# A decoder layer with a retrieval FFN on one core: second-pass products behind the V sums, adaLN on 32-column tiles, a later cache fetch, longer rings, samples as a unit

## The reference

```python
sh1,sc1,g1,sh2,sc2,g2 = split6(silu(c) @ w_ada + b_ada)     # adaLN, c: 1 prompt row + 8 sample rows
h  = RMSNorm(x)*(1+sc1)+sh1
q,k,v,p,ga,gb = split(h @ w_in)                             # (520 tokens, 1024) @ (1024, 3328)
A  = window_attention(q, k, v)                              # window 128; samples: 128 cached keys each
B  = multiscale_pool(p)
x  = x + g1 * ((sigmoid(ga)*(A@w_a) + sigmoid(gb)*(B@w_b)) @ w_out)
h2 = RMSNorm(x)*(1+sc2)+sh2
# PEER: 8 heads; 16 of 128*128 experts per token and head
s_half, i_half = top_k(h2 @ w_q . sub_keys, 16)             # two halves of 128 keys
best, expert   = top_k(all 16x16 sums, 16)
act = gelu(h2 . u_tab[expert])                              # one row of 1024 per expert
x  = x + g2 * sum_over_heads_and_slots(softmax(best) * act * v_tab[expert])
```

## Time and profile before

| | before |
|---|---|
| median of 3 runs (lowest to highest) | 2025.64 us (2020.49 to 2031.15) |
| profiled execution, its own time | 2020.82 us |
| its span, first to last instruction | 2018.8 us |
| granted clock of TensorE, mean | 0.825 of full speed |
| busy: PE, DVE, POOL, ACT | 68%, 55%, 54%, 13% |
| DMA: moved, mean rate | 639.19 MB, 317 GB/s |

### The profile page before, as it was taken

How to read it: one execution, slowest core, us unless ns; L and a number is a source line. 1 busy time by engine, 2 the same in 40 slices (tenths; PEclk the granted TensorE clock), 3 DMA queues, 4 the chain that set the end, 5 groups by cost and what they waited for, 6 DMA issues and landing times.

```text
span 2018.8 us, 19410 instructions
## 1 busy us (share of the span) xinstructions
PE 1379.0 (68%) x7019; PEld 677.7 (34%) x7019; DVE 1108.1 (55%) x2614; ACT 257.1 (13%) x488; POOL 1093.1 (54%) x1066
## 2 busy tenths in 40 slices
PE   5799889998687766555887555555565555654577
PEld 2256746757344443232443111121111112111122
DVE  4111324137865665756466676667777765776521
ACT  2012531112111100111111000001000000100020
POOL 2100000005766657567477777757777775777772
PEclk9899899899798978778898667777666777678899
DMA  9422332469999989979699999989999998999994
GB/s 273 110 88 94 107 83 85 156 241 332 354 380 401 357 339 382 367 279 393 247 384 379 406 406 409 401 332 408 358 408 405 406 399 326 407 406 402 409 372 171
DMA packets 196264, 639.19 MB, mean 317 GB/s; under 512 B 21856, under 2 KB 23188, under 8 KB 196042
## 3 DMA queue, kind: packets, MB, share of 16 engines
q0 software_dynamic: 154992, 550.65, 70.6%
q1 hardware_dynamic: 41178, 87.30, 12.8%
HBM read 634.09 MB, written 3.59 MB: 316 GB/s over the span
## 4 chain that ended last, share of the span: by engine, by line
POOL 36%; PE 31%; DMA 13%; issue 13%; DVE 4%; ACT 2%; DVEq 0%; SPq 0%; POOLq 0%; ACTq 0%
POOL arena L491 36%; PE psum L1153 16%; DMA arena<-in_peer_v,arena 6%; PE psum L1453 5%; PE psum L1214 4%; DMA arena<-in_peer_u,arena 4%; DMA arena<-in_w_ada 2%; ACT arena L540 1%; PE psum L1462 1%; DVE arena L1044 1%; DMA arena<-in_x_sample 1%; PE psum L1507 1%; ACT arena L591 1%; PE psum L1241 1%; PE psum L1465 0%
## 5 line engine op out<-in xcount | busy, mean ns | idle before, releaser
L1453 PE MATMUL psum<-arena 64*64 64x512 f32 x4096 | 672.6, 808 | 490.9 <-DMA arena<-in_peer_v,arena 488.3
L1044 DVE CUSTOM_DVE_ANT_0 arena<-arena 128x1024 f32<-128x1024 f32 x512 | 624.4, 1225 | 455.4 <-DMA arena<-in_peer_u,arena 441.7
L491 POOL DMA_INDIRECT arena<-in_peer_u,arena x520 | 529.2, 1018 | 315.7 <-issue 154.5
L491 POOL DMA_INDIRECT arena<-in_peer_v,arena x520 | 538.3, 1035 | 277.4 <-issue 148.3
L1453 PEld LDWEIGHTS psum<-arena 64*64 64x64 f32 x4096 | 204.8, 178 | 934.5 <-issue 931.2
L1153 PE MATMUL psum<-arena 128*128 128x264 f32 (+3 forms) x1812 | 470.9, 419 | 44.3 <-DMA arena<-in_w_ada 19.5
L1153 PEld LDWEIGHTS psum<-arena 128*128 128x128 f32 (+1 forms) x1812 | 323.0, 184 | 186.4 <-issue 105.4
L540 ACT ACTIVATE arena<-psum 128x256 f32<-128x256 f32 (+10 forms) x217 | 89.5, 442 | 558.9 <-PE psum L1153 384.0
L676 ACT ACTIVATE arena<-arena 128x16 f32<-128x16 f32 x32 | 6.9, 217 | 879.4 <-DVE arena L1044 879.3
L1214 PE MATMUL psum<-arena 128*128 128x512 f32 (+3 forms) x240 | 88.5, 530 | 1.6 <-DVE arena L802 1.6
L780 DVE TENSOR_TENSOR arena<-psum,arena 128x36 f32<-128x36 f32 x12 | 2.4, 196 | 117.5 <-PE psum L1176 117.5
(11 more groups left out here) (196 smaller groups left out, 777.9 us busy)
## 6 DMA issues: line engine op xcount, KB each, us to landing
arena<-in_w_ada SPq DMA_DIRECT2D x12, 2048.0 KB, 9.8
arena<-in_w_in SPq DMA_DIRECT2D x10, 2048.0 KB, 10.6
arena<-in_peer_wq SPq DMA_DIRECT2D x8, 2048.0 KB, 9.5
arena<-in_peer_u,arena POOLq DMA_INDIRECT x520
arena<-in_peer_v,arena POOLq DMA_INDIRECT x520, 6.7
arena<-in_w_out SPq DMA_DIRECT2D x4, 2048.0 KB, 14.0
arena<-in_w_branch_attn SPq DMA_DIRECT2D x4, 1024.0 KB, 11.6
arena<-in_w_branch_pool SPq DMA_DIRECT2D x2, 2048.0 KB, 10.7
```

Of the source, the lines that this page charges most:

```text
L491: pool.indirect_dma_start(out=row, out_offset=None, in_=table[0], in_offset=bass.IndirectOffsetOnAxis(ap=index, axis=0)).then_inc(landed, 16)
L1044: dve.tensor_tensor_reduce(row, row, h2n[b], 1.0, 0.0, ALU.mult, ALU.add, acts[:, u % 2, r % TOPK:r % TOPK + 1]).then_inc(u_used, 1)
L1453: ins = pe.matmul(psum[i * HW:(i + 1) * HW, 2 * g + h, :], diags[n % 4][ps, k + i, :], v_rows[(r + i) % V_RING][ps, h * 512:(h + 1) * 512] ...
```

## The change

What it does, part by part. (1) In TensorE's loop the second-pass steps of a half unit stand behind its `combine`; the steps' numbers move (`AT_O2` 24 to 26; the norm's parts, which were all at 32, are at 36 to 39; `AT_H2N` 35 to 41; `AT_PQ` 36 to 42), and the sums of squares are taken step by step. (2) `ada_products` writes its 8 matmuls to four column groups of 32, two to a group; `scT` is 32 columns wide with zeros, and `ada` adds the four groups while it turns them, by a matrix of four stacked identities (`K_SEL`). (3) POOL waits for the third `w_ada` product before it issues the constants, `w_pool` and the cache fetch; the fold's constants come later still. (4) From place 18 on each ring has 10 buffers (`ring_table`), the four new ones in weight slots that are free by then. (5) The samples are a place of their own, the 28th of 33 (`SAMPLES_AT` = 27), with 8 rows; their sum, their output and its store come ahead of the last block's. (6) `fold` writes banks 4 and 5 (for block 0 two banks of the plan) and stands one pair of half units later; a new block's `combine` waits for `sums_scaled`, which DVE raises, and no more for ACT's copy.

```diff
-U_RING, V_RING = 6, 6
-AT_A, AT_B, AT_O2, AT_NORM, AT_H2N, AT_PQ = 8, 16, 24, 32, 35, 36
+RING_ROWS, MORE_ROWS = 6, 4
+MORE_UNIT = 18
+SAMPLES_AT = 27
+PLACES = UNITS + 1
+AT_A, AT_B, AT_O2, AT_SK, AT_SS, AT_MEAN, AT_NORM, AT_H2N, AT_PQ = 8, 16, 26, 36, 37, 38, 39, 41, 42
...
+def ring_table(rows, first, more_from, more):
+
+    queue, buf, before, landing, used = [(i, None) for i in range(first)], [], [], [], {}
+    for r in range(rows):
+        if r == more_from:
+            queue = [(first + i, None) for i in range(more)] + queue
+        i, last = queue.pop(0)
+        queue.append((i, r))
...
-        pool.dma_start(kc[:, P:], consts[:, P:K_FOLD]).then_inc(consts_loaded, 16)
-        pool.dma_start(halves_on, consts[:, K_FOLD:K_END]).then_inc(fold_loaded, 16)
+        wait_filled(pool, ("ada_rows", 2))
+        pool.dma_start(kc[:, K_IOTA:], consts[:, K_IOTA:K_FOLD]).then_inc(consts_loaded, 16)
...
+        for p in range(2, PLACES):
             for q in range(4):
-                v_gathers(u, q)
-                u_gathers(u + 2, q)
+                v_gathers(p - 2, q)
+                u_gathers(p, q)
...
+            if AT_O2 + 3 <= k < AT_O2 + C + 2:
+                c = k - AT_O2 - 2
+                dve.wait_ge(squares_ready, C + c + 1)
+                ins = dve.tensor_tensor(squares1[:, 0, :], squares1[:, 0, :], squares1[:, c, :], ALU.add)
...
+            if k == AT_MEAN:
+                mean_squares(2, 1)
             if k == AT_NORM:
-                dve.wait_ge(squares_ready, 2 * C)
-                dve.tensor_tensor(squares1[:, 0, :], squares1[:, 0, :], squares1[:, C - 1, :], ALU.add).then_inc(square_sum_ready, 1)
-                mean_squares(2, 1)
-            if k == AT_NORM + 1:
                 normalize(3, half(1))
...
             if b:
-                dve.wait_ge(rows_folded, b)
+                dve.wait_ge(y_ready, b)
...
         def ada_products(i):
 
             w = chunk(("ada", i))
-            end(product(begin(("ada_rows", i))[0:9, :], [(scT[:, k, :], w[:, k, :]) for k in range(8)]))
+            o = begin(("ada_rows", i))
+            for k in range(8):
+                ins = pe.matmul(o[k % 4 * 32:(k % 4 + 1) * 32, :], scT[:, k, :], w[:, k, :], start=(k < 4), stop=(k >= 4), skip_group_check=True)
+            end(ins)
...
             if n % 16 == 0:
                 if b:
-                    pe.wait_ge(y_ready, b)
+                    pe.wait_ge(sums_scaled, 4 * b)
...
-        for n in range(2 * UNITS):
-            late_products(2 * n + 8)
-            late_products(2 * n + 9)
+        for n in range(2 * PLACES):
+            p, f = n // 2 + 2, n % 2
+            if (p, f) == (SAMPLES_AT - 1, 1):
+                pick_rows(0, 4)
+            if (p, f) == (SAMPLES_AT, 1):
+                pick_rows(4, S)
+            if p - 2 == SAMPLES_AT:
+                combine_samples(f)
+            else:
+                combine(unit_at(p - 2), f)
+            for k in (2 * n + 8, 2 * n + 9):
+                late_products(k)
...
-            combine(n // 2, n % 2)
-            if n % 16 == 15 and n < 2 * UNITS - 1:
-                fold(n // 16)
+            if n % 16 == 1 and 16 < n < 56:
+                fold(n // 16 - 1)
```

More of the change, by code:

```diff
@@ L163, in bank_plan @@
             plan += [(("sc", i, 1), "A"), (("scs", i), "A")]
-    return plan
+        if m == 1:
+            plan += [(("rows", 0, h), "A") for h in both]
+    return plan
+def ring_table(rows, first, more_from, more):
[5 more added lines that the diff above has]
+        queue.append((i, r))
+        used[i] = used.get(i, 0) + 1
+        buf.append(i)
+        before.append(last)
+        landing.append(16 * used[i])
+    return buf, before, landing
 def weight_chunks():
@@ L503, in v_gathers, with index_of @@
-        def v_gathers(u, q):
-            for r in range(u * TOPK + q * GS, u * TOPK + (q + 1) * GS):
-                b, i = slot(r)
-                if r >= V_RING and r % 2 == 0:
-                    pool.wait_ge(v_used, r - V_RING + 2)
-                gather(peer_v, v_rows[r % V_RING], eidx[:, b, i:i + 1], v_landed[r % V_RING])
-        for u in range(2):
+        def index_of(p, r):
+            if p == SAMPLES_AT:
+                t = r - sample_row(0)
+                return idx_s[:, t:t + 1]
+            b, i = slot(unit_at(p))
+            i += r - row(unit_at(p), 0)
+            return eidx[:, b, i:i + 1]
@@ new lines, in u_gathers @@
+        def u_gathers(p, q):
+            if q == 0 and p == SAMPLES_AT:
+                pool.wait_ge(sample_routed, 1)
+            elif q == 0:
+                pool.wait_ge(routed, unit_at(p) + 1)
+            if (p, q) == (MORE_UNIT, 0):
+                wait_filled(pool, ("pq", 15, 1))
+            for r in quarter(p, q):
+                if u_before[r] is not None:
+                    pool.wait_ge(u_used, u_before[r] + 1)
+                gather(peer_u, u_rows[u_buf[r]], r, index_of(p, r), u_landed[u_buf[r]])
@@ L511, in _, with v_gathers @@
+        def v_gathers(p, q):
+            for r in quarter(p, q):
+                if v_before[r] is not None and r % 2 == 0:
+                    pool.wait_ge(v_used, v_before[r] + 2)
+                gather(peer_v, v_rows[v_buf[r]], r, index_of(p, r), v_landed[v_buf[r]])
+        for p in range(2):
             for q in range(4):
[L512 to L513 removed]
+                u_gathers(p, q)
+        for p in range(2, PLACES):
             for q in range(4):
[L515 to L516 removed]
@@ L531, in _ @@
+                u_gathers(p, q)
+        for p in range(PLACES - 2, PLACES):
+            for q in range(4):
+                v_gathers(p, q)
         pool.wait_ge(windows_stored, 16 * 6)
@@ L1444, in combine @@
             for k in range(0, 8, 2):
-                r = 8 * n + k
-                first, last = r % SLOTS == 0, r % SLOTS == SLOTS - 2
-                for i in range(2):
-                    pe.wait_ge(v_landed[(r + i) % V_RING], 16 * ((r + i) // V_RING + 1))
+                first, last = n % 16 == 0 and k == 0, n % 16 == 15 and k == 6
+                pair = [row(u, 8 * f + k + i) for i in range(2)]
+                for r in pair:
+                    pe.wait_ge(v_landed[v_buf[r]], v_landing[r])
                 for h in range(2):
@@ new lines, in fold, with pick_rows @@
+            if b:
+                ins.then_inc(rows_folded, 1)
+        def pick_rows(first, end_t):
+            for t in range(first, end_t):
+                for h in range(2):
+                    if t:
+                        pe.wait_ge(sample_h_used, 2 * t + h - 1)
+                    else:
+                        pe.wait_ge(sample_x_used, 2)
+                    pe.matmul(psum[:, 6 + h, :], pick_s[:, t, :], h2n[NB][:, h * 512:(h + 1) * 512],
+                              start=True, stop=True).then_inc(sample_h_ready, 1)
```

306 lines of the change are left out of this document (163 added, 143 removed).

## The result

| | before | after |
|---|---|---|
| median of 4 runs (lowest to highest) | 2027.14 us (2020.49 to 2031.15) | 1949.12 us (1943.87 to 1951.54) |
| ratio, 95% interval | | 0.9615 (0.9581 to 0.9649) |
| span of the profiled execution | 2018.8 us | 1949.7 us |

The change makes the kernel faster by 3.9%. 1885 was forecast, and 1949 lies above the range's 1930. The span is 69.1 us shorter where the sum had 138.5. Where the rest went is read in the order of the prediction's terms. First the dense stage: TensorE's instructions in order, answering to the earlier trace rows, and POOL's first gather, answering to the earlier trace rows.

What follows compares the result with a forecast made beforehand. TensorE or its waits bound the dense stage to 455 us, the DMA engines the retrieval stage; 2020.8 - 38 - 20 - 10.5 - 56 - 14 = 1882, set at 1885 us for the runs' median, range 1850 to 1930.

Steps and rivals of the forecast that it cites:

- the start: Before the first projection: it begins at 45 instead of 82.8 us, a gain of 38 us (30 to 43).
- the fetch: Start: k and v cache fetch, issued behind the third adaLN product, no longer delays the fourth chunk; k took 54.1 us.
- The column tiles: adaLN products on four overlapping 32-column tiles: 1.95 instead of 7.04 us each; chance of no overlap 0.07, giving 1921.
- The estimate of 2.2 us: adaLN product time by the skill page, scaled from three column tiles measured 2.38 times as fast to four.
- The end: Behind the last V rows: 14 of 28.1 us remain, a gain of 14 us (12 to 15).
- `ada` 8 to 11: Dense stage, two pairs of adaLN products: half the possible gain taken, as chunks limit it, 10.5 us (9 to 13).
- the new wait: Second pass: DVE waits for products now behind sums, 8 or 9 us each half unit, mostly fitting its slack; cost 5 us.
- 58 to 70%: DVE's busy share in the retrieval stretches, read as room for the wait for products behind the sums.
- The gain at the block borders: Retrieval stage: sums not behind products, spread norm, later folds, longer rings and moved samples give back 61 us.
- DVE is made late: Rival, second pass: products behind sums run partly at half clock, 4 us for each of about 15 half units: 1945; chance 0.10.
- half clock: Path of the late-DVE rival: half of 48 matmuls behind the sums at half the clock, some 6 us more.
- the DMA engines set the stage's pace: Retrieval stage, first gather to about 1991 us: DMA-bound, 406 GB/s undisturbed, 1.3 us for each 512 KB gather.

Runs made afterwards that it cites:

- products first: The changed kernel with the second-pass products of a half unit put back ahead of its sums on TensorE, all else as changed: 1901.34 us, 0.9393.
- e2_after_one_input: The changed kernel with each DVE dot replaced by a sum over the U row alone, the product with the token row left out: 1897.67 us, one run.

## Why the prediction was wrong

**Right: the start** (38 forecast, 35.8 measured) and its main cause, the fetch. **The column tiles** overlap (1.95 forecast, 1.92 measured, four tiles 3.7 times as fast as in a row). The estimate of 2.2 us by the Trainium skill ("TensorE: Matmul & The Clock Gate", Part 3) is further off. **The end** (14 forecast, 12.1 measured). `ada` 8 to 11 were mis-sized (10.5 forecast, 3.3 measured), as the chunks' landing ends the waits and the products behind these waits take nearly twice as long, at a granted clock of 0.50 to 0.57.

**The step that failed** is the price of the new wait: "the wait fits on the whole; I leave 5 us". The size of each wait was near (8 or 9 us forecast, 5 to 13 measured, 10.1 on the mean), and DVE had idle time too. Its waits for U rows, 400 to 1140 us (total, times, longest), with the change and then with products first:

```profile
DVE arena L1121 <- DMA arena<-in_peer_u,arena: 129.2, 65, 6.6
```

```profile
DVE arena L1121 <- DMA arena<-in_peer_u,arena: 214.9, 94, 10.0
```

So some 86 of the 121 us fitted into idle time. The other 35 made DVE late, which is about as much as POOL's waits for U rows grew (39). And the idle time that took the 86 was not free. DVE's dots, spread out by the landing of their rows, left POOL gaps; pushed together behind a wait they don't: 144 gathers start within the first 0.75 us of a dot with the change, 98 with products first. The 46 more, by an estimate of 0.7 to 0.8 us each, are most of the 40 us by which the gathers are longer. Measured, the order costs 48 us beside the other parts (1949 for 1901), and by the table above 79 of U waits and longer gathers against 30 of V waits. The prediction looked at DVE's time alone, and put the held gathers at nothing. Its reading of that time was also too even: by the earlier trace rows DVE is busy 77% of the first stretch (65.70 of 85 us) and 53% of the one at 850 us, not 58 to 70%.

**The gain at the block borders** was right in kind. With products first the stage is 1488.1 us (first gather at 396.74, last sums at 1884.88), 47 under before's, where 61 were forecast ahead of the 5. It was not the order that brought it: fold banks, spread steps, samples and rings did together, of which only the rings were undone by themselves (29 us), and the order's own V gain overlaps with theirs.

**The rivals.** "DVE is made late" gave 1945, with a chance of 0.10, and has the place right. Its path was another, and its nearness to 1949 is chance: with the change, seven of the eight groups of 48 matmuls behind the sums take 10.96 us at a granted clock of 1.00, and the eighth 11.36 at 0.96, so no half clock takes part. A product starts only when the sums ahead of it have their last V rows, and is due before. That the DMA engines set the stage's pace was half of it: with gathers of 0.95 us the rate stays at 409 GB/s, 1.28 us for each 512 KB, so the limit is there. POOL with 1.24 us is 3% quicker, and each held gather costs it most of a microsecond that it doesn't win back soon.

Rates below the full one stand behind the second pass too, where no product is waited for. With the change, 1340 to 1440 and 1700 to 1850 us, and the same stretches with one-operand dots (`e2_after_one_input`):

```profile
1340.00:1440.00 100.00, 54.58 (x296) 16.43 (x288) 73.76 (x192) 6.11 (x9) 78.04 (x71) 0.69 0.99 372
1700.00:1850.00 150.00, 87.21 (x384) 22.87 (x376) 102.07 (x226) 9.00 (x12) 117.35 (x108) 0.70 0.99 379
```

```profile
1340.00:1440.00 100.00, 54.00 (x300) 17.67 (x304) 74.01 (x146) 6.11 (x9) 75.86 (x80) 0.78 1.03 409
1700.00:1850.00 150.00, 84.59 (x448) 24.86 (x448) 94.14 (x138) 9.22 (x13) 107.52 (x114) 0.74 1.02 405
```

With nothing held they run at 405 to 409 GB/s, so the low rates there are held gathers as well. Some of the order's price falls here: the last 440 gathers, all behind the second pass, take 588 us with the change and 576 with products first, and 570 in either order with one-operand dots. Left open: why the order, which moves nothing there, leaves more of them held.

Products first with everything else of the change is the quickest of the kernels that compute the whole layer, with the one that reads token rows from PSUM: 1901 and 1900 us.

## What to carry to other kernels

Two engines that wait for each other at two places share one loop: moving work behind a wait on one shifts the due time on the other, so price the order by who is late next, and undo each part alone, since two parts can shorten the same wait. Read a DMA stage by the instruction that issues (count, time of one, gap, waits); a share of DMA time near 1 also stands over stretches at 322 GB/s. Idle time between the instructions of an engine that isn't the bound can be what another engine runs in.

## What was not expected of the hardware

An indirect gather issued on GpSimd in the first 0.75 us of a 1.22 us reduction of 128x1024 on VectorE with both operands in SBUF is held until that ends. The two in the rows above end 0.81 us behind the reduction's end, as the median of all such gathers in the changed kernel does; they take 1.3 to 2.0 us, for 0.94. With one operand in SBUF (0.95 us), or one in PSUM (0.94), it is not. The Trainium skill ("SBUF — State Buffer", Who interferes with whom) has the rule: a VectorE instruction with two SBUF inputs contends with a GpSimd instruction that reads SBUF, and one with at most one does not, outside certain modes. These runs agree, with 1.71 for 0.94 us. The same section says that `tensor_tensor` did not stall DMAs in a probe, and infers that making descriptors needs a port which such an instruction leaves free. Here a two-input reduction does lengthen gathers, whose indices lie in SBUF.
